# Input projection of a hybrid attention and recurrence block: token-major banks that end one by one, a narrower shared-key tile, tokens loaded first

## The reference, cut to what matters

```
h = rmsnorm(x, g_pre)                      # (2048, 1024)
proj = h @ w_in                            # columns: c_q 768, c_kv 256, k_pe 32, gate_a 512,
                                           # hq 512, hf 512, hi 512, gate_b 512, merge 2048
q  = rmsnorm(c_q) @ w_uq ;  kv = rmsnorm(c_kv) @ w_ukv
k_pe = apply_rope(k_pe)                    # one 32-wide rotary key, shared by 8 heads
x1, x2 = k_pe[:16], k_pe[16:]              # rope: [x1*cos - x2*sin, x1*sin + x2*cos]
attn = chunk_causal_attention(q, [k_nope, k_pe], v)
o = hgrn2_chunkwise(hq, 1 - f, hi, log f)
y = merge of both branches @ w_out;  x + rmsnorm(y)
```

## Time and profile before

| | us |
|---|---|
| median of three runs (2346.69, 2347.9, 2352.19) | 2347.9 |
| the profiled execution, its own device time | 2347.51 |
| its span, from the first to the last instruction | 2345.7 |
| mean granted clock of PE, share of full speed | 0.976 |

### The profile page before, as it was taken

One profiled execution on the slowest core, in us unless ns is written; L12 is line 12 of the kernel. 1 busy time (PEld: TensorE's weight loads), 2 busy tenths in 40 slices (PEclk: granted clock), 3 DMA queues, 4 the chain that ended last, 5 costly groups with the idle time before them and its releaser, 6 DMA issues. The chain is left out here.

```text
span 2345.7 us, 32911 instructions
## 1 busy us (share of the span) xinstructions
PE 2204.9 (94%) x11601; PEld 1823.9 (78%) x11601; DVE 1044.2 (45%) x1866; ACT 903.9 (39%) x1676; POOL 301.8 (13%) x200
## 2 busy tenths in 40 slices
PE   6999999989997999999978889999999998999998
PEld 5888888768776888888866767778888777778886
DVE  6111000010004544444536647777777776564652
ACT  7221111010013444444434325565666666453441
POOL 1222215031301111111100000000000014200000
PEclk9999999999998999999989989999999999999999
DMA  5222132131212322333238774333113326574751
GB/s 181 86 69 76 59 86 77 45 142 55 90 54 85 93 86 89 98 98 94 84 133 272 244 226 113 70 70 72 38 40 72 72 80 204 179 221 131 210 152 64
DMA packets 217763, 258.65 MB, mean 110 GB/s; under 512 B 39792, under 2 KB 138512, under 8 KB 215184
## 3 DMA queue, kind: packets, MB, share of 16 engines
q1 hardware_dynamic: 192720, 210.32, 31.9%
q10 hardware_dynamic: 23808, 43.03, 4.9%
q0 software_dynamic: 1152, 4.19, 0.5%
HBM read 159.41 MB, written 98.07 MB: 110 GB/s over the span
## 5 line engine op out<-in xcount | busy, mean ns | idle before, releaser
L74 PE MATMUL bankD<-hT_hi,shared_w_hi 128*128 128x512 f32 x512 | 212.4, 415 | 11.5 <-POOLq L830 11.5
L74 PE MATMUL bankA<-hT_hi,shared_w_hi 128*128 128x512 f32 x544 | 213.3, 392 | 0.0
L75 PE MATMUL bankA<-hT_lo,shared_w_hi 128*128 128x512 f32 x544 | 212.1, 390 | 0.0
L76 PE MATMUL bankA<-hT_hi,shared_w_lo 128*128 128x512 f32 x544 | 212.1, 390 | 0.0
L76 PE MATMUL bankD<-hT_hi,shared_w_lo 128*128 128x512 f32 x512 | 201.7, 394 | 0.0
L75 PE MATMUL bankD<-hT_lo,shared_w_hi 128*128 128x512 f32 x512 | 200.9, 392 | 0.0
L1791 DVE TENSOR_REDUCE small_chunk_min<-scores 128x1 f32<-128x512 f32 (+2 forms) x320 | 181.4, 606 | 39.8 <-PE scores L76 20.4
L1811 ACT ACTIVATE probs<-scores,small_least 128x1024 f32<-128x1024 f32 (+2 forms) x192 | 167.3, 871 | 12.8 <-DVE small_least L1798 11.6
L74 PE MATMUL bankA<-wt_hi,hT_hi 128*128 128x512 f32 x384 | 152.7, 398 | 13.2 <-DVE shared_v_raw L485 7.7
L75 PE MATMUL bankA<-wt_lo,hT_hi 128*128 128x512 f32 x384 | 150.7, 393 | 0.0
L76 PE MATMUL bankA<-wt_hi,hT_lo 128*128 128x512 f32 x384 | 150.6, 392 | 0.0
(11 more groups left out here) (250 smaller groups left out, 4592.5 us busy)
## 6 DMA issues: line engine op xcount, KB each, us to landing
projT<-stage ACTq DMA_DIRECT2D x68, 256.0 KB, 2.4
shared_w_raw<-in_w_in_dram SPq DMA_DIRECT2D x32, 512.0 KB, 4.4
projT<-d_stage ACTq DMA_DIRECT2D x64, 256.0 KB, 2.4
e_l_in<-projT SPq DMA_DIRECT2D x64, 256.0 KB, 5.0
gateTok<-stage ACTq DMA_DIRECT2D x32, 256.0 KB, 2.0
shared_w_lo<-hgTok SPq DMA_DIRECT2D x16, 512.0 KB, 3.4
knT<-b_out SPq DMA_DIRECT2D x32, 256.0 KB, 3.4
vTok<-b_out SPq DMA_DIRECT2D x32, 256.0 KB, 3.0
```

Source lines behind the costliest of these rows:

```text
L74: pe.matmul(out, a_hi, b_hi, start=first, stop=False)
L75: pe.matmul(out, a_hi, b_lo, start=False, stop=False)
L76: return pe.matmul(out, a_lo, b_hi, start=False, stop=last)
```

## The change

Four things are changed in the input projection, and one in the latent stage.

1. SP loads token tiles 0 and 1 ahead of the identity and the gain. ACT no longer waits for these at its start, and issues a root of a constant first; the wait for the identity and gain comes before its first rounding.
2. The very first half that PE turns goes tile by tile: four transposes of tile 0 when that tile is normalised, then of tile 1, and so on. All other halves stay as they were.
3. The shared-key tile has only the key's 32 columns, loaded once. POOL writes their high part in columns 0 to 31 and their low part in columns 32 to 63 of one stationary tile of 64 columns. PE multiplies it by `hT_hi` and by `hT_lo`: two matmuls in place of three for each k and block. Rows 0 to 31 and 32 to 63 of the result are stored apart, and the latent stage loads both (24 DMAs instead of 16) and adds them on DVE (64 x 1024 elements) before the rotation.
4. Token-major: k = 0 to 5 run as before; k = 6 and 7 run together for each bank, so that a bank gets its last six matmuls in a row and the banks end six matmuls apart. POOL waits for the whole earlier segment before k = 6 too.

```diff
+        TM_LAST = 2
@@ SP
-                sp.dma_start(ident[:], ident_d).then_inc(const_in, 16)
-                sp.dma_start(gain[:], ...).then_inc(const_in, 16)
...
                         sp.dma_start(x_tile[g % 2][:, j], x[t * P:(t + 1) * P, :]).then_inc(x_in[g % 2][j], 16)
+                        if t == 1:
+                            sp.dma_start(ident[:], ident_d).then_inc(const_in, 16)
+                            sp.dma_start(gain[:], ...).then_inc(const_in, 16)
...
-                sp.dma_start(w_raw[:, 0, :, 0:QK], w_v[:, :, C_PE - NOPE:C_PE + ROPE]).then_inc(w_in_s[0], 16)
-                sp.dma_start(w_raw[:, 0, :, QK:QK + 16], w_v[:, :, C_PE + 16:C_PE + 32]).then_inc(w_in_s[0], 16)
-                sp.dma_start(w_raw[:, 0, :, QK + 16:P], w_v[:, :, C_PE:C_PE + 16]).then_inc(w_in_s[0], 16)
+                sp.dma_start(w_raw[:, 0, :, 0:ROPE], w_v[:, :, C_PE:C_PE + ROPE]).then_inc(w_in_s[0], 16)
@@ POOL
-                split_tile(0, T_PE, T_PE // 2 * 16 + 48)
+                pool.wait_ge(w_in_s[0], T_PE // 2 * 16 + 16)
+                pool.wait_ge(fm_done, T_PE * NB + NB)
+                pool.tensor_scalar(w_hi[:, 0, :, 0:ROPE], w_raw[:, 0, :, 0:ROPE], 1.0, None, ALU.mult).then_inc(w_hi_ready, 1)
+                pool.wait_ge(w_hi_ready, T_PE + 1)
+                pool.tensor_tensor(w_hi[:, 0, :, ROPE:2 * ROPE], w_raw[:, 0, :, 0:ROPE], w_hi[:, 0, :, 0:ROPE].bitcast(F32), ALU.subtract)\
+                    .then_inc(w_ready, 1)
...
-                        if k < KD - 1:
-                            pool.wait_ge(wt_used, s * (KD - 1) + (k + 1))
+                        if k < KD - TM_LAST:
+                            pool.wait_ge(wt_used, s * (KD - TM_LAST) + (k + 1))
                         else:
                             pool.wait_ge(tm_done, s * TT + TT)
@@ ACT
-                act.wait_ge(const_in, 32)
                 act.wait_ge(const_set, 2)
+                act.activation(std[:, 0:1], ones[:, 0:1], ACT.Sqrt, bias=eps[:, 0:1], scale=1.0).then_inc(std_ready, 1)
+                act.wait_ge(std_ready, 1)
...
+                    if g + half == 0:
+                        act.wait_ge(const_in, 32)
                     act.wait_ge(xT_done, 2 * g + half + 1)
@@ PE, first turn
+                    if g + half == 0:
+                        for j in range(TPB):
+                            pe.wait_ge(xn_ready, j + 1)
+                            for k in ks:
+                                last = turn(k, j)
@@ PE, shared key
-                tile_products(0, T_PE)
+                pe.wait_ge(w_ready, T_PE + 1)
+                for blk in range(NB):
+                    pe.wait_ge(bank_free, T_PE * NB + (blk + 1))
+                    cols = slice(blk * BLK, (blk + 1) * BLK)
+                    for k in range(KD):
+                        for part, h in enumerate((hT_hi, hT_lo)):
+                            last = pe.matmul(bank[0:2 * ROPE, blk], w_hi[:, 0, k, 0:2 * ROPE], h[:, k, cols], start=k + part == 0,
+                                             stop=k + part == KD)
+                    last.then_inc(fm_done, 1)
@@ PE, token-major
-                        for k in range(KD):
+                        for k in range(KD - TM_LAST):
                             if half == 0:
                                 pe.wait_ge(wt_ready, s * KD + (k + 1))
                             for b in range(8):
...
+                                last = products(k, b)
+                            if half == 1:
+                                last.then_inc(wt_used, 1)
+                        if half == 0:
+                            pe.wait_ge(wt_ready, s * KD + KD)
+                        for b in range(8):
+                            for k in range(KD - TM_LAST, KD):
+                                last = products(k, b)
+                            last.then_inc(tm_done, 1)
@@ latent stage, SP and DVE
-                        rows = slice(NOPE + part * HALF_ROPE, NOPE + (part + 1) * HALF_ROPE)
-                        sp.dma_start(k_x[to, part], projT[T_PE, rows, cols]).then_inc(k_in, 16)
+                        for low in range(2):
+                            rows = slice(low * ROPE + part * HALF_ROPE, low * ROPE + (part + 1) * HALF_ROPE)
+                            sp.dma_start((k_x, k_t)[low][to, part], projT[T_PE, rows, cols]).then_inc(k_in, 16)
                         sp.dma_start(k_cs[to, part], rope_d[row:row + HALF_ROPE, cols]).then_inc(k_in, 16)
...
-                    dve.wait_ge(k_in, 16 * 4 * NB)
+                    dve.wait_ge(k_in, 16 * 6 * NB)
+                    dve.tensor_tensor(k_x[:], k_x[:], k_t[:], ALU.add).then_inc(k_step, 1)
+                    dve.wait_ge(k_step, 1)
```

More of the change, by code:

```diff
@@ L182, in _ @@
             def _(sp):
-                sp.dma_start(ident[:], ident_d).then_inc(const_in, 16)
-                sp.dma_start(gain[:], g_pre.rearrange("o (k p) -> p (o k)", p=P),
-                             allow_slow_non_contiguous=True).then_inc(const_in, 16)
                 def load_next_constants():
@@ L367, in latent_rows_out, with tile_out @@
                     act.dma_start(rsTok, c_rstd[:, 0:TT]).then_inc(c_stored, 16)
-                def tile_out(n, u, func, sums=False):
+                def tile_out(n, u, func, sums=False, rows=P):
                     for blk in range(NB):
@@ L372, in tile_out @@
                         act.wait_ge(stored[blk], n * 16 + 16)
-                        src = bank[:, u * NB + blk]
+                        src = bank[0:rows, u * NB + blk]
                         if isinstance(n, int) and n < N_LORA:
                             latent_square(n, blk, src)
-                        act.activation(stage[:, blk], src, func).then_inc(bank_free, 1)
+                        act.activation(stage[0:rows, blk], src, func).then_inc(bank_free, 1)
                         act.wait_ge(bank_free, n * NB + (8 + blk + 1))
-                        act.dma_start(projT[ds(n, 1), :, blk * BLK:(blk + 1) * BLK].rearrange("o p n -> (o p) n"),
-                                      stage[:, blk]).then_inc(stored[blk], 16)
+                        act.dma_start(projT[ds(n, 1), 0:rows, blk * BLK:(blk + 1) * BLK].rearrange("o p n -> (o p) n"),
+                                      stage[0:rows, blk]).then_inc(stored[blk], 16)
                         if sums and blk < NB - 1:
@@ L398, in _ @@
                         tile_out(i * 2 + (T_HF + u), u, ACT.Sigmoid)
-                tile_out(T_PE, 0, ACT.Copy)
+                tile_out(T_PE, 0, ACT.Copy, rows=2 * ROPE)
                 act.wait_ge(lb_step, 2)
@@ L494, in turn_half, with turn @@
                 def turn_half(g, half):
-                    pe.wait_ge(xn_ready, g * TPB + TPB)
-                    for k in range(half * KD // 2, (half + 1) * KD // 2):
-                        if g + half:
+                    ks = range(half * KD // 2, (half + 1) * KD // 2)
+                    def turn(k, j):
+                        return pe.transpose(bank[:, B_XT + k % 4, j * P:(j + 1) * P],
+                                            x_tile[g % 2][:, j, k * P:(k + 1) * P], ident[:])
+                    if g + half == 0:
[3 more added lines that the diff above has]
+                                last = turn(k, j)
+                    else:
+                        pe.wait_ge(xn_ready, g * TPB + TPB)
+                        for k in ks:
                             pe.wait_ge(hT_lo_ready, g * KD + (k - 3))
-                        for j in range(TPB):
-                            last = pe.transpose(bank[:, B_XT + k % 4, j * P:(j + 1) * P],
-                                                x_tile[g % 2][:, j, k * P:(k + 1) * P], ident[:])
+                            for j in range(TPB):
+                                last = turn(k, j)
                     last.then_inc(xT_done, 1)
@@ L578, in _, with products @@
                     for half in range(2):
-                        for k in range(KD):
+                        def products(k, b):
+                            t = half * 8 + b
+                            if k == 0:
+                                pe.wait_ge(tm_free, s * TT + (t + 1))
+                            rows = slice(t * P, (t + 1) * P)
+                            return three_products(pe, bank[:, b], (hT_hi[:, k, rows], hT_lo[:, k, rows]),
+                                                  (wt_hi[:, k], wt_lo[:, k]), k == 0, k == KD - 1)
+                        for k in range(KD - TM_LAST):
                             if half == 0:
@@ L582, in _ @@
                             for b in range(8):
-                                t = half * 8 + b
-                                if k == 0:
-                                    pe.wait_ge(tm_free, s * TT + (t + 1))
-                                rows = slice(t * P, (t + 1) * P)
-                                last = three_products(pe, bank[:, b], (hT_hi[:, k, rows], hT_lo[:, k, rows]),
```

(7 more changed lines are left out.)

10 lines of the change are left out of this document (7 added, 3 removed).

## The result

The changed kernel takes 2331.67 us (median of 4 runs, 2331.15 to 2333.51) where the kernel before takes 2347.36 (median of 4 runs, 2346.69 to 2352.19). The ratio is 0.9928 with a 95% interval of 0.9914 to 0.9943. It is faster, by 15.7 us where the sum said 25.4. The interval of the ratio leaves 1 out, but the gain is under one per cent.

What follows compares the result with a forecast made beforehand. PE, with work in 94% of the span, plus the gaps in front of it was taken as the bound; 2.7 + 7.2 + 11.9 + 3.0 + 4.2 - 3.6 = 25.4 us gave about 2322 us, range 2315 to 2331.

Steps and rivals of the forecast that it cites:

- the wide range: Whole kernel: 2315 to 2331 us, to hold the time 8 times in 10, rivals up to 2330 taken in.
- the forecast's own range: Whole kernel: 2318 to 2326 us around the forecast of about 2322, given 0.57.
- Tokens first: Start: second group's first tile lands 0.9 us earlier, ACT rounds at 16.3 instead of 19.07; gain 2.7 us (1.9 to 3.5).
- Shared key: Feature-major part, shared-key tile: 32 of 96 matmuls go at 0.2265 us each; gain 7.2 us (6.4 to 8.5).
- the estimate of another 0.7 us: Shared-key tile: 64 matmuls would give back 0.7 us more if weight loads cost by their columns; not in the sum.
- Half changes and clock: Token-major: PE's waits at begun banks mostly go, 11.9 us gained; half-clock matmuls behind them go, 3.0 us gained.
- The rival of the store ring: Token-major values: k = 7's load slows the stores, 4.6 us back and the clock falls as before; time 2330, chance 0.13.
- End of the stage: End of token-major: ACT keeps up with banks ending 1.36 us apart; gain 4.2 us (3 to 4.5).
- New waits of POOL: Token-major, seventh group: PE waits for splits of k = 6 and 7; cost nothing, with 27 us of cover.
- Latent stage: Latent stage: SP's 8 added DMA issues delay ACT, DVE and PE; cost 3.6 us (0 to 8).
- the rival that it costs nothing: Latent stage: the key's second half costs nothing, PE's waits at DVE being short; time 2318.5, chance 0.15.
- its reverse: Latent stage: the key's second half costs 8 us; time 2326.5, chance 0.08.

Runs made afterwards that it cites:

- e1: Kernel before with parts 1 and 2 of the change alone (token loads first, early root, first half turned tile by tile): 2349.3 us, ratio 1.0008.
- e10: On top of e9, SP loads the second group of token tiles ahead of the first two weight tiles: 2318.16 us, ratio 0.9865.
- e6: On top of e4, POOL begins its first weight split only after DVE has scaled two tiles of the second group: 2327.29 us, ratio 0.9916.
- e2: Kernel before with part 3 alone (narrow shared-key tile, its two halves loaded and added later): 2346.81 us, ratio 0.9997.
- e11: On top of e9, a third buffer for the value tiles, in the stage tile: 2318.11 us, ratio 0.9866.
- e5: On top of e4, SP's load of the second segment's weights k = 7 moved behind the stores of value tiles 8 to 15: 2328.19 us, ratio 0.9917.
- e3: Kernel before with part 4 alone (token-major k = 6 and 7 together for each bank): 2332.65 us, ratio 0.994.
- e4: Changed kernel, with POOL's output-stage subtractions for w_out rows k = 0 to 3 held until DVE's gated product is done: 2327.4 us, ratio 0.9915.
- e7: On top of e4, the shared key's high and low rows loaded with one DMA instead of two, 16 instead of 24: 2325.63 us, ratio 0.9912.
- e9: Changed kernel with the edits of e4, e5 and e7 together: 2319.23 us, ratio 0.9874.

## Why the prediction came out as it did

The direction was right, and the mechanism of its largest terms. The gain was 15.7 us against 25.4. The time lies at the upper end of the wide range, 2331: 0.7 us above it as measured, and on it if the ratio is taken from the 2347.9 that the forecast started from. It is well above the forecast's own range of 2318 to 2326. That it came no worse than the wide range's end is partly luck, since 5.2 us of the loss lie in a stage that no step spoke of and that varies by some 5 us from one execution to the next. By its steps:

- **Tokens first: failed** (2.7 forecast; e1 gives 0.3, the changed kernel -0.4). "The loads run without a pause, so it lands 0.9 us earlier" was wrong. ACT takes the second group's first tile 0.5 us later than before. The load of the gain, in 4-byte pieces, landed at 3.8 us before, when no token had come yet; now it lies among the tokens and lands at 6.95. I had counted the issues of the two moved loads on SP, not their transfers. That these hold the tokens back is my reading; it was not tried alone. The rows fit it: the first tile lands 1.0 us earlier than before, the third, issued behind the two, 0.5 later. e10 shows the step's other half to be right: with that group early ACT rounds at 14.17. The second fault was to take ACT for the only way to the low part. DVE reaches it after two scalings, which POOL's splits stretch (e6: 0.76 against 1.58), so even the 1.4 us that ACT gained ended as 0.25. Nor does this part bring anything together with the narrow key: e2, without it, ends feature-major at 410.94, and the eight traces with both (e10 left out) at 411.3 to 412.0. Tile 3's root ended at 11.6 instead of 10.3, which cost nothing.
- **Shared key: right** (7.2; e2 gives 7.75 with the start's scatter). The 64 matmuls have their own row now, weight loads and matmuls of the one operand pair (ns shortest/median/longest, from start to end in us):

```profile
L597 PEld LDWEIGHTS bankA<-hT_hi,shared_w_hi x32: 134/134/135, 397.2 to 411.4; 128*64 128x64 f32 x32
L597 PE MATMUL bankA<-hT_hi,shared_w_hi x32: 387/397/398, 397.4 to 411.6; 128*64 128x512 f32 x32
```

  A weight load of 64 columns takes 134 ns; with 128 it was 190. Yet the matmuls follow each other every (411.87 - 397.38) / 63 = 0.230 us, not faster than the 0.2265 of the others. The Trainium skill, page "TensorE: Matmul & The Clock Gate", section "LDWEIGHTS (loading the stationary operand)", lets a load cost by its columns. Here it is shorter with half the columns, but not by half, and the estimate of another 0.7 us did not come true. That the longer load, at 190 ns, was hidden behind the matmuls already is likely, but was not tried by itself.
- **Half changes and clock: right in kind, 1.0 short** (14.9; 13.9). The waits are 3.0 us where I left 1.6 and 0.6, and the clock falls behind the second change, which the sum put at nothing and only the low end of that term foresaw ("0 if the residual ones still bring the clock down"). What there was to gain was larger than the 14.1 + 3.0 that I had summed: 19.7 us from 280.71 to e11's 261.02. The larger stake hides part of the two shortfalls. The rival of the store ring, 0.13, was partly right: the store of tile 8 is issued behind k = 7's load, and ACT waits 4.26 us for it. Its size was not: it had 4.6 us coming back and the clock falling at both changes. And e5 shows that this is not the whole mechanism. One store landing in 4.9 instead of 3.4 us does the same without that load. Nor does the clock always fall behind such a wait: e3 and e4 have the same wait (1.9 and 1.8 us) at the second change and no slow matmuls behind it. What decides that is open.
- **End of the stage: right** (4.2; 4.3).
- **New waits of POOL: right**, no wait of PE at a seventh group.
- **Latent stage: right in size, and that the added loads are what costs** (3.6; 3.8). e7 takes out the 8 issues and gets 3.8 back, so the rival that it costs nothing and its reverse both fall. The sum on DVE takes 1.21 us (forecast 1.4) and is mostly hidden, as the step said.
- **What no step named:** 2.0 us around `bankD`, and 5.2 in the output stage. `bankD` starts behind 7.2 us of idle PE, and 12 of its matmuls go at half clock where 9 did before. That costs nothing yet: PE stands at the next wait, for POOL, 9.58 us after its first `bankD` matmul, before 9.59. But the 24 small matmuls behind that wait now go at half clock too, as these rows and windows of the changed kernel and then of the kernel before show:

```profile
697.57 2.82 PE L1094 MATMUL bankD<-d_qd,d_ki 64*128 64x128 f32 x24 [1.90 <-POOL d_qd L862]
697.57:700.32 2.75, 2.75 (x24) 2.63 (x24) 0.00 (x0) 0.00 (x0) 0.00 (x0) 0.50 0.43 110
```
```profile
722.56 1.55 PE L1060 MATMUL bankD<-d_qd,d_ki 64*128 64x128 f32 x24 [1.90 <-POOL d_qd L828]
722.56:724.04 1.48, 1.48 (x24) 1.41 (x24) 0.00 (x0) 0.00 (x0) 0.00 (x0) 0.99 0.20 55
```

  Those 1.3 us account for `bankD`'s 1.1. The 0.8 ahead of `bankB` was not traced; this stretch has 14.7 to 15.5 us in the traces at hand. Of the output stage's 5.2, about 2.5 are DVE's products behind POOL (the fourteen traces, four with long products and ten without, do not overlap there), and the rest lies within what this stage varies by from one execution to the next. "The time is PE's own plus the gaps in front of it" held, but I took the stages behind as a rigid block that only moves. Which of two engines comes first there differs between the traces, and I take the shifted arrival times to be the reason; no experiment moved them alone.

## What to carry to other kernels

Cost a moved transfer by what it transfers and among what it then runs, not by its issue, and follow every engine that feeds the next step, not just the first. Buffers that go round just fast enough for the mean store wait on the slow one; a third buffer took every wait out of this stage (6.0 us against e9's trace), where moving the load that delayed one store (e5) brought none. When a change shifts the times at which stages begin, look for pairs of DVE and POOL operations that start within a microsecond: here they cost about 2.5 us, more than the tokens-first part brings. And where executions of one kernel differ by 10 us, read a stage from several traces before giving it a cause.

## What the runs showed of the hardware

- DVE's product of 128x512 with both inputs in SBUF takes 0.69 us alone and 2.73 to 2.84 when a subtraction of POOL began just before it; with DVE first, POOL's 2.39 become 2.85. A scaling of 128x1024 takes 0.75 us alone and up to 2.67 beside POOL's splits (e10).
- Stores of the same 512 KB landed in 2.6 to 4.9 us in these traces. A late one brought a wait of 1.8 us, and behind it, in some traces but not in e3 and e4, seven or eight matmuls at half clock.
- Behind the 7.2 us of idle PE ahead of `bankD` matmuls go at half clock, and 24 small ones took 2.82 us at a granted clock of 0.50 where they took 1.55 at 0.99.
- A weight load of 64 columns takes 134 ns against 190 for 128, without a faster stream of matmuls of 512 columns.
- The attention stage, the same instructions in every kernel here, took 567.4 to 573.6 us with a granted clock of 0.97 or 0.98.
